# Five convolution iterations in seven block products, with the weight sums on GpSimd

## The reference

```
u = rmsnorm(x);  proj = u @ w_in            # 4096 x 24576, ten slices
a_q a_f a_i a_g : gated linear recurrence (HGRN2), 16 heads   -> y_a (2048)
c_b c_c c_h c_g : y_b = c_b * conv3(c_c * c_h) * silu(c_g)    -> y_b (2048)
z_a = y_a @ w_branch_a;  z_b = y_b @ w_branch_b               # 2048 x 4096 each
merged = sigmoid(g_a + bias_a) * z_a + sigmoid(g_b + bias_b) * z_b
out = rmsnorm(x + merged @ w_out)           # 4096 x 4096
```

## Time and profile before

| what | value |
|---|---|
| median of 3 runs | 2886.66 us (2886.27 to 2888.61) |
| profiled execution | 2887.28 us, its span 2885.6 us |
| granted TensorE clock | 0.998 of full |
| TensorE busy | 2849.9 us (99%) |
| VectorE busy | 1982.4 us (69%) |
| ScalarE busy | 1319.7 us (46%) |
| GpSimd busy | 6.7 us |
| moved by DMA | 564 MB, 196 GB/s |

### The profile page before, as it was taken

How to read it: one execution, slowest core, us unless ns; L and a number is a source line. 1 busy time by engine, 2 the same in 40 slices (tenths; PEclk the granted TensorE clock), 3 DMA queues, 4 the chain that set the end, 5 groups by cost and what they waited for, 6 DMA issues and landing times.

```text
span 2885.6 us, 38782 instructions
## 1 busy us (share of the span) xinstructions
PE 2849.9 (99%) x12935; PEld 2357.6 (82%) x12935; DVE 1982.4 (69%) x2209; ACT 1319.7 (46%) x1420; POOL 6.7 (0%) x22
## 2 busy tenths in 40 slices
PE   8999999999999999999999999999999999999998
PEld 7888888888888788888887888888888888888776
DVE  6566766676667645555469686776868777886886
ACT  5443444344444444333445454454545445554554
POOL 0000000000000000000000000000000000000000
PEclk9999999999999999999999999999999999999999
DMA  7555555555555556655556666666666666766655
GB/s 236 184 178 168 173 176 175 169 173 179 175 170 175 187 192 193 191 190 189 189 182 204 199 221 200 212 209 204 214 200 218 199 214 206 240 202 215 213 203 204
DMA packets 416844, 564.20 MB, mean 196 GB/s; under 512 B 25745, under 2 KB 288002, under 8 KB 416770
## 3 DMA queue, kind: packets, MB, share of 16 engines
q1 hardware_dynamic: 416770, 563.25, 60.5%
HBM read 555.28 MB, written 7.86 MB: 195 GB/s over the span
## 4 chain that ended last, share of the span: by engine, by line
PE 94%; DVE 3%; DMA 1%; issue 1%; DVEq 1%; ACT 1%; SPq 0%; ACTq 0%
PE PS L1315 21%; PE PS L1317 21%; PE PS L1316 21%; PE QL L1442 7%; PE QL L1441 7%; PE QL L1440 7%; PE PS L1440 2%; PE PS L1442 2%; PE PS L1441 2%; PE QL L1346 2%; DMA RP<-in_w_out 1%; DVE QS L1079 1%; DVE QS L722 1%; DVEq L701 1%; PE QL L1323 0%
## 5 line engine op out<-in xcount | busy, mean ns | idle before, releaser
L722 DVE TENSOR_TENSOR QS<-RP,QS 128x1024 fp32r<-128x1024 f32 x716 | 872.7, 1224 | 732.2 <-ACT QS L444 715.8
L444 ACT ACTIVATE QS<-RP 128x1024 fp32r<-128x1024 f32 x716 | 755.8, 1059 | 1105.1 <-PE PS L1317 987.2
L1315 PE MATMUL PS<-QS,U 128*128 128x512 f32 x2176 | 860.2, 395 | 10.0 <-DVE QS L722 7.4
L1317 PE MATMUL PS<-QS,U 128*128 128x512 f32 x2176 | 849.4, 390 | 0.0
L1316 PE MATMUL PS<-QS,U 128*128 128x512 f32 x2176 | 848.6, 390 | 0.0
L1315 PEld LDWEIGHTS PS<-QS,U 128*128 128x128 f32 x2176 | 409.7, 188 | 96.1 <-issue 7.9
L1317 PEld LDWEIGHTS PS<-QS,U 128*128 128x128 f32 x2176 | 409.2, 188 | 86.8
L1316 PEld LDWEIGHTS PS<-QS,U 128*128 128x128 f32 x2176 | 409.9, 188 | 81.4
L1440 PE MATMUL QL<-QS,U 128*128 128x512 f32 x964 | 376.1, 390 | 3.3 <-DVE GA L1207 3.3
L1442 PE MATMUL QL<-QS,U 128*128 128x512 f32 x964 | 375.8, 390 | 0.0
L1441 PE MATMUL QL<-QS,U 128*128 128x512 f32 x964 | 375.7, 390 | 0.0
(11 more groups left out here) (252 smaller groups left out, 2127.3 us busy)
## 6 DMA issues: line engine op xcount, KB each, us to landing
RP<-in_w_in SPq DMA_DIRECT2D x1024, 256.0 KB
RP<-in_w_in SPq DMA_DIRECT2D x256, 512.0 KB
RP<-in_w_out SPq DMA_DIRECT2D x128, 512.0 KB
RP<-in_w_branch_a SPq DMA_DIRECT2D x64, 512.0 KB
RP<-in_w_branch_b SPq DMA_DIRECT2D x64, 512.0 KB
XS<-in_x SPq DMA_DIRECT2D x8, 512.0 KB, 5.5
XR<-in_x SPq DMA_DIRECT2D x16, 256.0 KB, 4.5
out_dram<-H SPq DMA_DIRECT2D x8, 512.0 KB, 3.9
```

Of the source, the lines that this page charges most:

```text
L444: act.activation(WS[s][:, :, 0:OW], RAW[s][:, :, :], ACT.Copy).then_inc(hi_ready, 1)
L722: dve.tensor_tensor(WS[s][:, :, OW:2 * OW], RAW[s][:, :, :], WS[s][:, :, 0:OW], ALU.subtract).then_inc(lo_ready, 1)
L1315: pe.matmul(bank, top, w[:, k, 0:OW], start=at_k == 0, stop=False)
L1317: op = pe.matmul(bank, low, w[:, k, 0:OW], start=False, stop=at_k == n_tiles - 1)
```

## The change

The convolution iterations 3 to 7 (five of eight) now use the plan of the gates, with 7 of 16 pairs in seven block products. The four sums are formed by GpSimd, in these iterations and in all eight gate products; the output projection keeps its sums on VectorE. Since the four column slices now end together, the results are combined after the product with an overlap into the next one: ScalarE copies banks out, VectorE adds the common terms, and the gate's sigmoid and the three products follow. A raw chunk is loaded by two DMAs of 256 KB, and in RP[0] the first half of each chunk waits for the sum that reads it last (t_sum) and not only for lo_ready. The activation sums (seven_sums) move to convolution iteration 2.

```
+FIRST_SEVEN = 3
+CONVS = NP - FIRST_SEVEN
...
 # SyncE
+            def load_gates(i, k, c, chunk, sum_done):
...
+                for g in range(2):
+                    if g == 0 and sum_done is not None:
+                        sp.wait_ge(t_sum, sum_done)
+                    if g == 1 or sum_done is None:
+                        sp.wait_ge(lo_ready, chunk - (RING - 1))
+                    sp.dma_start(RAW[s][:, g, :], src[:, g, bass.ds((i + 1) * OW - OW, OW)]).then_inc(raw_loaded[s], 16)
...
 # GpSimd
+            def weight_sums(chunk0, used, u):
+                chunk, n = chunk0 + 2 * u, GATES.first[u]
+                s = 2 * u % RING
+                w12, w11, w22, w21 = [RP[s // 2][:, q, :] for q in range(4)]
+                sums = [QF[:, (n + 3 + q) % QRING, OW:2 * OW] for q in range(4)]
+                for t in (s, s + 1):
+                    pool.wait_ge(raw_loaded[t], (chunk - s) * (16 * KC // RING) + 16 * KC)
+                for q, (x, y) in enumerate(((w11, w12), (w22, w12), (sums[0], w22), (sums[2], w21))):
+                    pool.wait_ge(block_used, used + (n + 3 + q - QRING + 1))
+                    op = pool.tensor_tensor(sums[q], x, y, ALU.add)
+                    if q >= 2:
+                        op.then_inc(t_sum, 1)
+                    if q in (1, 2):
+                        pool.drain()
...
 # ScalarE, after the product of a convolution iteration
+                act.activation(TX[:, 1, :], PS[0][:, 0, :], ACT.Copy).then_inc(a_out, 1)
+                for c in range(RING):
+                    if c == 2:
+                        act.wait_ge(front_done, i + (1 - FIRST_SEVEN))
+                        act.activation(GA[:, :, :], QL[:, 0:2, :], ACT.Copy).then_inc(front_out, 1)
+                    if c == 3:
+                        act.wait_ge(w_used, chunk + 2 * CD)
+                        act.activation(GB[:, :, :], QL[:, 2:4, :], ACT.Copy).then_inc(back_out, 1)
+                    next_hi(GATES, chunk, used, c)
+                act.wait_ge(front_summed, i + (1 - FIRST_SEVEN))
+                act.activation(SIG, CSF[:, :, :], ACT.Sigmoid).then_inc(gate_sig, 1)
...
 # VectorE: the sums leave seven() where given=True (gates and convolution)
+                if not given:
...
+            def conv_seven(i):
...
+                    if kind == "S":
+                        seven(GATES, chunk, used, sums, u, n_th, given=True)
+                    else: ... plain(GATES, chunk, u, h)
+                    if u in (3, 5):
+                        convolve(i - 1, (u - 1) // 2)
...
+                dve.tensor_tensor(TX[:, 0, :], c, TX[:, 1, :], ALU.add)
+                dve.tensor_tensor(TX[:, 1, :], d, TX[:, 0, :], ALU.add)
+                ... lo of next chunks 0 and 1
+                dve.tensor_tensor(GA[:, :, :], GA[:, :, :], TX[:, :, :], ALU.subtract)
+                ... GA[:, b, :] += e, twice; lo of next chunk 2
+                dve.tensor_tensor(GB[:, 0, :], a, GB[:, 0, :], ALU.add)
+                dve.tensor_tensor(GB[:, 1, :], GB[:, 1, :], TX[:, 1, :], ALU.add).then_inc(drained, 1)
+                ... lo of next chunk 3
+                dve.tensor_tensor(CSG[:, :, :], CSG[:, :, :], CK[:, :, :], ALU.mult)
+                dve.tensor_tensor(CF[:, :, :], CF[:, :, :], CSF[:, :, :], ALU.mult)
+                dve.tensor_tensor(CF[:, :, :], CF[:, :, :], SIG, ALU.mult).then_inc(drained, 1)
...
 # TensorE
-            with pe.Fori(2, NP) as i:
-                branch(i, CONV_CHUNK, CONV_GROUP, is_conv=True, conv_of=i - 1)
+            branch(2, CONV_CHUNK, CONV_GROUP, is_conv=True, conv_of=1)
...
+            conv_seven(FIRST_SEVEN, first=True)
+            with pe.Fori(FIRST_SEVEN + 1, NP) as i:
+                conv_seven(i)
```

More of the change, by code:

```diff
@@ new lines, in conv_seven @@
+            def conv_seven(i, first=False):
+                chunk, sums = CONV_CHUNK + BRANCH * i, sums_at(i - FIRST_SEVEN)
+                n_th = 0
+                for u, (kind, j) in enumerate(GATES.units):
+                    sum_done = sums - 1 if u == 0 and not first else None
+                    if u >= 2 and GATES.units[u - 2][0] == "S":
+                        n_th += 1
+                        sum_done = sums + (2 * n_th - 1)
+                    for h in range(2):
+                        load_conv(i, j + KH * h, 2 * u + h, chunk + 2 * u + h, None if sum_done is None else sum_done + h)
@@ L548, in block_free, with seven @@
                     act.wait_ge(block_used, used + (n - QRING + 1))
-            def seven(plan, chunk0, used, sums, u, n_th):
+            def seven(plan, chunk0, used, sums, u, n_th, conv_of=None):
                 chunk, n = chunk0 + 2 * u, plan.first[u]
@@ L574, in plain, with product_hi @@
                 op.then_inc(hi_ready, 1)
-            def product_hi(plan, chunk0, used, sums):
+            def product_hi(plan, chunk0, used, sums, conv_of=None):
                 n_th = 0
@@ L582, in product_hi @@
                     if kind == "S":
-                        seven(plan, chunk0, used, sums, u, n_th)
+                        seven(plan, chunk0, used, sums, u, n_th, conv_of if n_th == 0 else None)
                         n_th += 1
@@ L1054, in _, with seven @@
             branch(1, CONV_CHUNK, is_conv=True, conv_of=0, norm=True)
[L1055 to L1059 removed]
+            branch(2, CONV_CHUNK, is_conv=True, conv_of=1, unscaled=True, last=True)
+            def seven(plan, chunk0, used, sums_at, u, n_th, given=False):
@@ L1460, in plain @@
                         pe.wait_ge(lo_ready, chunk + h + 1)
-                    if first and m == 2 and back_drained is not None:
-                        pe.wait_ge(drained, back_drained)
+                    if m == 0 and front is not None:
+                        pe.wait_ge(*front)
+                    if m == 2 and back is not None:
+                        pe.wait_ge(*back)
+                    if m == 2 and between is not None:
+                        between()
                     for b in range(2):
```

216 lines of the change are left out of this document (153 added, 63 removed).

## The result

| | before | after |
|---|---|---|
| median, us (lowest to highest, runs) | 2886.47 (2885.54 to 2888.61, 4) | 2985.38 (2982.77 to 2987.35, 4) |
| ratio to before | 1 | 1.0341 [1.0323, 1.0359] |
| span of the profiled execution, us | 2885.6 | 2981.0 |
| one of the convolution iterations 3 to 7, us | 87.96 | 93.4 |
| a merge, us | 127.1 | 136.2 |

The change makes the kernel 98.9 us slower. 76.7 us were predicted (2963 us), with the cause: GpSimd and VectorE in turn, and a loop through RP[0] that no longer closes.

What follows compares the result with a forecast made beforehand. The number of matmuls on TensorE was taken to bound the kernel. Matmuls -23.8, S-pair intervals +84.5, convolution pieces +11 and joints +5 gave +76.7 us on 2887.3, so a median of 2963 us; range 2861 to 3030.

Steps and rivals of the forecast that it cites:

- a loop through RP[0]: S pairs: sums, drains, issue and next load take 9.8 us against TensorE's 10.2; any hold over 0.4 us lengthens it.
- What bounds it, and the matmuls (-23.8 us): Number of matmuls on TensorE bounds the kernel; 21 fewer per convolution iteration save 4.76 us, 23.8 us for five.
- In turn: GpSimd adds and VectorE's two-input SBUF subtractions exclude each other, 6.6 + 4.7 = 11.3 us in a 10.2 us pair; chance 0.62.
- Price of a sum: One GpSimd add of 128x512: 1.17 us, bounds 0.95 to 1.38; four sums 4.7 us for each S pair.
- The interval from S to S: From one S pair to the next: 11.5 us, between 11.3 (both engines' sum) and 12.1 (loop), 1.3 over TensorE's pace.
- The gates: Gate products in the eight merges: each loses 6.5 us, from six S-to-S intervals of 1.3 us less remaining slack.
- what is left of the slack at the first: First S pair of a product: 3.2 us early minus about 1.9 of queueing leaves 1.3 us to deduct.
- The convolution iterations: Five iterations: matmuls save 23.8 us; 6.5 us lost per product, 11 us behind VectorE's convolution pieces, 5 us at the joint.
- The joint: Between two convolution products: transposes and first S pair come about 1 us late, 5 us for five iterations.
- A: Rival: GpSimd and VectorE don't disturb each other, the loop stays at 9.8 us, total 2864 us; chance 0.22.
- B: Rival: no disturbance, but an add costs 1.38 us, loop 10.6, total 2878 us; at 1.45 us 2889; chance 0.09.
- C: Rival: an add costs 2 us or more for its own reasons, loop 13.1 us, total 3073 us; chance 0.07.

Runs made afterwards that it cites:

- e3: The changed kernel with each GpSimd add replaced by two memsets of the same tile with a drain between, sums left out: 2856.73 us.
- e5: The changed kernel with all sums on VectorE and the convolution cut into five pieces instead of two: 2865.54 us.
- e8: The kernel before with 301 unneeded 128x384 GpSimd adds, inputs from an SBUF constant, during the first recurrence iterations: 2913.74 us.
- e4: The changed kernel with the raw quarters of RP[0] released one by one for the next loads: 2987.3 us.
- e7: As e3, but three memsets with drains for each sum instead of two, sums left out: 2956.55 us.
- e6: The changed kernel with two of the four sums (q0, q1) on GpSimd and q2, q3 on VectorE: 2930.76 us.

## Why the prediction was right, and where its sizes were off

**What bounds it, and the matmuls (-23.8 us): right.** 83.2 us for a convolution iteration in e3 and 83.8 in e5, where 83.2 were worked out. Two readings behind it were off and change nothing: all waits of TensorE in that view add up to 24.0 us and not to some 14, which is the sum of the three lines shown, and the stretch of 782 us holds 6.2 merges.

**In turn: right, and it is the cause, with the loop that carries it on.** With memsets (e3) GpSimd's instructions and VectorE's subtractions keep their durations. With adds VectorE's lo of the raw blocks goes from 1.75 to 2.37 us in the mean, and sums take up to 2.8 us. That was the rule of the Trainium skill (SBUF — State Buffer, Who interferes with whom), that a VectorE instruction with two inputs in SBUF and a GpSimd instruction that reads SBUF exclude each other. By that rule the trace agrees: the third sum above takes 2.56 us beside line 1194, e8 stretches the instructions with two inputs in SBUF, and it leaves alone the one that reads PSUM (747 ns in both).

**Price of a sum: 1.17 us predicted, 1.28 to 1.30 measured.** It lay in the bounds (0.95 to 1.38). The three streams are not all in turn, but closer to it than the middle. The estimate of 1.12 us that was worked out from the figure of the Trainium skill (GPSIMD Engine Reference, Elementwise side-by-side) is 13% short of the 1.28 us.

**The interval from S to S: 11.5 us predicted, 11.3 to 11.4 measured.** Both ways to work it out had been meant as bounds, the sum of both engines (11.3) and the loop with line 1079 inside (12.1). The runs show two limits that stand at nearly the same place. Shorten the loop, and the two engines in turn are at 11.15 us (e4). Take the shared reading away and keep the loop about as long (7.45 + 3.8 = 11.2 us in e7 against 6.9 + 4.5 = 11.4 in after), and the merges stay at 136 us (e7). Corrected for the dearer sum, VectorE and GpSimd together are 6.6 + 5.2 = 11.8 us, a little more than the interval, so their instructions must overlap by some tenths of a us; where they do was not looked into.

**The gates: +52 us predicted, +72.9 measured; this is the term that was mis-sized.** A product loses 6.5 us in the prediction and 136.2 - 127.1 = 9.1 us in the trace. Counted in merge 1 by the starts of TensorE's matmuls beyond the 0.2267 us of its pace: 0.3 us at the first S pair, 6.8 us at the other six (1.13 each), and 1.9 us at the end. Two of the steps behind it failed, and the third went the other way:
- "less what is left of the slack at the first ... 1.3": nothing is left. The first S pair is already 0.3 us late. That is 1.6 us too few in a product.
- "So 6 intervals from S to S" as all that a product loses: the lateness goes on into the branch projections, whose first matmul waits 1.61 us for line 839 (1759.89 above). VectorE is behind by then, and has two parts of the gate's results (lines 1273 and 1275) ahead of that lo. It is 1.9 us that the sum lacked.
- The interval itself was 0.2 us shorter: 7.8 us were counted for the six and these starts give 6.8, 1.0 us too many.

6.5 + 1.6 + 1.9 - 1.0 = 9.0 us, against 9.1; over eight merges it is the missing 20 us.

**The convolution iterations: near.** They go from 87.96 to 93.4 us, +27 us for five, where -23.8 + 32.5 + 11 + 5 = +24.7 had been predicted. Against the 83.2 us without a loss, 10.2 us are lost in each (predicted 9.7). The joint shows as predicted, but at twice the price. The wait of the transposes in front of turn_conv (start us, us; VectorE's last instruction before it, and TensorE's first):

```profile
1164.44 1.59 DVE L1252 TENSOR_TENSOR GA<-GA,TX 128x512 f32<-128x512 f32 x1
...
1166.09 0.66 PE L1537 MATMUL PS<-IDN,GA 128*128 128x128 f32 x4 [1.91 <-DVE GA L1252]
```

It is 10.1 us over five instead of 5. Line 1252 needs 692 ns in the kernel e5, in the row shown there, and 1593 ns here. The other two terms were too large. In the iteration from 1166.09 on, by the starts of TensorE's matmuls, 2.2 us are lost at the joint (1.0 predicted) and 7.5 us at the S pairs, 1.9 and 1.0 of them at the two behind the pieces of the convolution (6.5 + 2.2 = 8.7 predicted for the S pairs and the pieces together). Which of those two terms holds the 1.2 us too many these starts can't tell.

**The rivals.** A (no disturbance, 2864 us) is e3, which left the sums out and came to 2856.7 us: the mechanism of A is right if GpSimd doesn't read. The 7 us between them are in part a gain that I had not counted. In the kernel before, two matmuls at 1519.36 and 1550.64 start 2.0 and 0.3 us behind TensorE's pace, at the joint between the last convolution iteration and the first merge. In e3 both delays are gone; that this is because the convolution's results are ready earlier is argued and not tested. Another 1.6 us lie in the seven distances between the merges and 1.5 us behind the last of these starts; why, the runs don't tell. The rest of the 7 us I can't place. B and C (the price alone) fall with e3, whose 4.9 us for four sums cost nothing, and with the 1.3 us that were measured. B's number for an add of 1.38 us without disturbance has not been tried as such; its second number is a slip, since by its own formula an add of 1.45 us gives a loop of 10.9 us and 2902 us, not 2889.

**What stays open.** What the loop alone would cost with adds of 1.3 us that nothing holds up can't be had here: e7 is longer (7.45 us) than the four sums with their gaps (5.2 + 0.4). With a load of 3.8 us (e7) to 4.5 us (after) these would make 9.4 to 10.1 us, an estimate by which the loop would just close and the holding up of the sums, to 6.9 us, is what opens it. That both are limits is shown; which ends last in one given pair is read from a timeline and changes from pair to pair.

**The version to take** is e5. It keeps the seven products, puts the sums back on VectorE and cuts the convolution into five pieces: 2865.54 us, 20.9 us faster than before and 119.8 us faster than the change.

## What to carry to other kernels

Work moved to an idle engine is free only if that engine takes nothing that the busy one needs; a run in which it does as much but reads nothing (e3) tells the price of its time from the price of its traffic. When a buffer comes to be released by another engine, add up the whole loop (work, issue, load) against the pace of the engine that bounds, and follow the lateness into the next stage: a fifth of the loss was found there. Before moving work off a busy engine, try to cut what stands in front of it into pieces shorter than its lead (e5).

## What the runs showed of the hardware

- One-input copies from SBUF to SBUF on VectorE are stretched as well: 230 to 540 ns for 256 elements (line 876 of before, line 883 of e8), though they have only one input.
- A GpSimd memset of the same tile (0.53 us, 728 of them in e3, 1092 in e7) leaves VectorE's instructions with two inputs in SBUF alone: 1757 and 1224 ns with it, 1752 and 1218 ns before. It does stretch some that read one tile in SBUF and write one: the first taps from 348 to 479 ns in the mean in e3 and 524 in e7, and the copy that rounds the convolution's result (line 1087 of e3, line 970 of before) from 428 to 505 and 550 ns. The taps that lie beside memsets for most of their time take 0.70 us, twice their 0.35.
- After a stall of TensorE its clock is sometimes granted at the lower of its two levels (1.2 instead of 2.4 GHz) for a short stretch. In before, after a wait of 2.41 us that ended at 969.05, the matmuls start 0.43 us apart from 970.35 on and 0.23 us apart again from 973.73 on. Eight matmuls at 0.2 us more are 1.6 us on top of the wait. It doesn't follow each time: in after the wait at the same place (2.44 us, to 969.06) is followed by a granted clock of 1.00 up to 978, and in e6 one of 1.89 us has such a stretch behind it. Two stretches of before, in and behind it (PE, PEld, DVE, ACT, POOL busy, PE clock, DMA share, GB/s):

```profile
970.40:973.60 3.20, 3.20 (x9) 2.55 (x8) 0.86 (x1) 0.00 (x0) 0.00 (x0) 0.50 0.78 242
975.00:978.20 3.20, 3.20 (x16) 2.65 (x15) 1.56 (x2) 1.60 (x3) 0.00 (x0) 1.00 0.34 102
```
